# Norm and step sizes as one stage, with three of its pieces taken from the attention stage

## The chip, the cores and the metric

One core of a Trainium2 chip runs the whole kernel. The metric is the device time of one execution in microseconds (us). Times of work inside an execution come from one profiled execution of the same kernel, counted from the start of its span.

## The reference, cut to what matters

The kernel computes one layer of an encoder for two sequences (256 and 512 tokens, 768 in all, model width 1024), all in float32:

```python
h = rmsnorm(x, norm_mix)
proj = h @ w_in                     # 1024 x 8768
q, k, v, z, xbc, dt_f, dt_b, gate_a, gate_s = jnp.split(proj, split_points, axis=-1)
dt = jax.nn.softplus(dt_raw + dt_bias)
a_cum = jnp.cumsum(dt * a_head)     # per head, within chunks of 128 tokens, both directions
attn = window_attention(rope(q), rope(k), v, sink)
a_out = attn @ w_out_attn
s_out = ssd_branch(z, xbc, dt_f, dt_b, ...) @ w_out_ssm
x = x + (sigmoid(gate_a) * a_out + sigmoid(gate_s) * s_out) @ w_o
x = x + hier_moe(rmsnorm(x, norm_ffn), ...)
```

What matters here is the head of it: the norm `h`, the step sizes `dt` with their running sums, and when the columns of `w_in` are multiplied.

## The kernel before, in words

**Stages.** The program is a row of stages: norm and transpose, step sizes, the SSD scan (four groups), attention, the output projections, and the mixture of experts. Each stage is a block in which every engine has its own list of instructions, written out by hand in program order; engines wait for each other through semaphores only. A stage ends with a barrier of all engines. TensorE, VectorE (DVE), ScalarE (ACT), GpSimd (POOL) and SyncE (SP, which issues most DMAs) each run their list strictly in the order written, so an instruction that waits holds back all that is behind it.

**Pieces.** `w_in` is multiplied in pieces of 128 columns (512 KB). A piece is loaded by SP (`load_piece`), its rounded high part is made by ACT (`round_piece`, L518), its low part by POOL (`lower_piece`, L523), and TensorE then forms high by high, low by high and high by low for the eight blocks of 128 rows (`products`, L185): 24 matmuls for the 256 tokens of the first sequence and 24 for the 512 of the second. Three pieces are in flight (`RING`). TensorE waits for a piece's low part with `pieces.ready`. Pieces come in two kinds. Those of `xbc` feed the scan at once. Side pieces (q, k, v, z and the gates, 44 in all) are stored to the DRAM tensor `projected` and read later. Before, 33 of the 44 side pieces are computed in the SSD stage and 11 in the attention stage.

**Norm and transpose.** Six tiles of 128 tokens. Per tile, ACT sums squares (L262), POOL makes the root, DVE scales (`scaled`, L303), TensorE transposes eight 128x128 blocks into two banks of PSUM (L331), DVE multiplies by the gain (`norm_hT`, L317, one instruction for each half of the features), ACT rounds (`h_high`, L273) and POOL subtracts (`h_low`, L294).

**Step sizes.** A stage of its own, so it begins when the last tile has left POOL. TensorE multiplies the 64 step columns with `h` (L185, 48 matmuls), ACT copies the result (L410), six small transposes follow (L382), then DVE and ACT compute softplus and log (L437 to L448), TensorE forms the sums (L389 to L396), DVE copies them out (L454 to L463), and SP stores them to `decay_sums` (L369). The SSD stage waits for that store. The first three pieces of `xbc` are loaded, rounded and lowered beside this chain.

**Attention.** After an opening with rotary work, the loop runs over 24 groups (a tile and one of 4 key heads, 4 query heads each). In group g TensorE issues scores of group g+1 for two heads, then one third of a side piece (`unit`, L531: 24 matmuls of 256 columns or 12 of 512), then scores for the other two heads, then for each head of group g transposes of probabilities (L1233) and products with the values (L1183). Scores alternate between two banks, so a head waits until DVE has read the head two before it:

```python
                        if m >= 2:
                            pe.wait_ge(s_read, m - 1)
```

The 11 side pieces are 33 units: 9 in the opening and one in each of the 24 groups.

Of the kernel before, what the change touches and what calls it, by code (L numbers as in the profile page):

```python
# [14 lines left out]
P = 128  # L15
# [46 lines left out]
SIDES, LAST_SIDES = 9, 6  # L62
SSD_SIDES = (SG - 1) * SIDES + LAST_SIDES
# [161 lines left out]
def norm_and_transpose(core):  # L225
# [5 lines left out]
    AHEAD = 3  # L231
    with own:
# [5 lines left out]
        hT = [sb(f"norm_hT{u}", [P, 4, P]) for u in range(2)]  # L238
        x_in = [sem(f"x_in{n}") for n in range(len(LOADS))]
        const_in, mean_ok, rstd_ok = sem("const_in"), sem("mean_ok"), sem("rstd_ok")  # L240
        h_ok, tr_done, gained, high_ok, low_ok = (
            sem("h_ok"), sem("tr_done"), sem("h_gained"), sem("h_high_ok"), sem("h_low_ok"))
        with nc.Block() as block:

            @block.sync
            def _(sp):
# [5 lines left out]
                sp.dma_start(core.w_dt[:, :, :], core.w_in_cols(DT0, 2 * SH)).then_inc(core.w_dt_in, 16)  # L252

            @block.scalar
            def _(act):
# [9 lines left out]

                for t in range(AHEAD):
                    squares(t)
                for t in range(NT):
                    if t + AHEAD < NT:
                        squares(t + AHEAD)  # L270
                    for j in range(2):
                        act.wait_ge(gained, 2 * t + j + 1)
                        act.activation(core.h.high[:, 4 * j:4 * j + 4, t * P:(t + 1) * P], hT[j][:, :, :],  # L273
                                       ACT.Copy).then_inc(high_ok, 1)

            @block.gpsimd
            def _(pool):
# [10 lines left out]
                for t in range(NT):  # L288
                    if t + AHEAD < NT:
                        roots(t + AHEAD)  # L290
                    for j in range(2):
                        pool.wait_ge(high_ok, 2 * t + j + 1)
                        at = (slice(None), slice(4 * j, 4 * j + 4), slice(t * P, (t + 1) * P))
                        pool.tensor_tensor(core.h.low[at], hT[j][:, :, :], core.h.high[at].bitcast(F32),  # L294
                                           ALU.subtract).then_inc(low_ok, 1)

            @block.vector
            def _(dve):
# [8 lines left out]
                scaled(0)  # L307
                for t in range(NT):
                    if t + 1 < NT:
                        scaled(t + 1)  # L310
                    for j in range(2):
                        n = 2 * t + j
                        dve.wait_ge(tr_done, n + 1)
                        if n >= 2:
                            dve.wait_ge(low_ok, n - 1)
                        gain = core.feat[:, P_GMIX + 4 * j:P_GMIX + 4 * j + 4]
                        dve.tensor_tensor(hT[j][:, :, :], core.bank[n % 8][:, :].rearrange("p (k t) -> p k t", k=4),  # L317
                                          gain.unsqueeze(2).to_broadcast([P, 4, P]), ALU.mult).then_inc(gained, 1)

            @block.tensor  # L320
            def _(pe):
                pe.sem_inc(core.pieces.done, 2 * RING)
                pe.wait_ge(const_in, 16)
                for t in range(NT):
                    pe.wait_ge(h_ok, t + 1)
                    for j in range(2):
                        n = 2 * t + j
# [162 lines left out]
def piece_column(n):  # L490

    if n < GC:
        return xbc_column(0, n)
# [2079 lines left out]
```

## Time and profile before

| | us |
|---|---|
| median of 3 runs (2049.47 to 2055.22) | 2050.53 |
| the profiled execution | 2054.24 |
| its span, first to last instruction | 2052.4 |
| norm and transpose, until the step sizes start | 34.7 |
| step sizes, until the first matmul of the SSD stage | 63.26 |
| loop of attention | about 835 to 1026 |

The stage times are read from the order of the instructions in the trace. Outside the span of the profiled execution lie 1.84 us.

### The profile page before, as it was taken

The page shows a single profiled execution, that of the slowest core. Times are in us where ns is not written, and L with a number is a line of the kernel's source. Part 1 is how long each engine was busy: PE and PEld are TensorE (multiplying, and loading weights), DVE is VectorE, ACT ScalarE, POOL GpSimd, SP SyncE. Part 2 cuts the span into 40 slices and gives each one's busy share as a digit, 9 for nine tenths or more (in the row PEclk, how much of TensorE's full clock was granted, in tenths as well). Part 3 has the DMA queues.
Part 4 walks back from the last instruction along what each step waited for, and adds up shares of the span by engine and source line. Part 5 has one row for each costly group of instructions (what it writes and reads, how often), then busy time and mean ns, then how long its engine had stood idle before and what let it go on. Part 6 is the DMA issues. An engine that isn't in the chain of part 4 may idle for free. (4 is left out here: it accounts for less than half of the span.)

```text
span 2052.4 us, 26125 instructions
## 1 busy us (share of the span) xinstructions
PE 1842.6 (90%) x9426; PEld 1420.9 (69%) x9426; DVE 1283.2 (63%) x1351; ACT 1006.8 (49%) x1579; POOL 639.4 (31%) x368
## 2 busy tenths in 40 slices
PE   4898999999999779899999898985999999999991
PEld 3777787787787645677888786444677777777771
DVE  2677866875884835433344354124888888888883
ACT  4244543533444431355675420122577787777761
POOL 5247646746754933100134431000010111111000
PEclk7999999999999978899999999986999999999996
DMA  3243452424335442231155444512899999999985
GB/s 110 66 128 91 118 141 80 129 85 131 109 107 147 134 160 57 70 126 37 44 183 168 145 154 150 229 72 84 302 355 374 372 375 366 378 370 372 375 301 199
DMA packets 228110, 379.50 MB, mean 185 GB/s; under 512 B 14576, under 2 KB 176624, under 8 KB 203312
## 3 DMA queue, kind: packets, MB, share of 16 engines
q1 hardware_dynamic: 220272, 363.45, 51.8%
q0 software_dynamic: 7168, 12.60, 1.8%
q10 hardware_dynamic: 576, 2.18, 0.3%
q8 instruction: 61, 1.00, 0.2%
q14 instruction: 33, 0.27, 0.0%
HBM read 333.94 MB, written 55.25 MB: 190 GB/s over the span
## 5 line engine op out<-in xcount | busy, mean ns | idle before, releaser
L2011 DVE TENSOR_TENSOR e_w_low<-e_raw,e_w_high 128x2048 fp32r<-128x2048 f32 x190 | 426.5, 2286 | 63.3 <-ACT e_w_high L2007 63.3
L523 POOL TENSOR_TENSOR w_w_low<-w_raw,w_w_high 128x1024 fp32r<-128x1024 f32 x92 | 250.4, 2722 | 456.0 <-ACT w_w_high L518 456.0
L2007 ACT ACTIVATE e_w_high<-e_raw 128x2048 fp32r<-128x2048 f32 x190 | 349.9, 1914 | 0.0
L185 PE MATMUL bank<-h_high,w_w_high 128*128 128x512 f32 (+1 forms) x912 | 320.7, 352 | 31.9 <-ACT ssd_conv_in L802 16.7
L185 PE MATMUL bank<-h_low,w_w_high 128*128 128x512 f32 (+1 forms) x912 | 312.2, 342 | 0.0
L185 PE MATMUL bank<-h_high,w_w_low 128*128 128x512 f32 (+1 forms) x912 | 311.7, 342 | 0.0
L185 PEld LDWEIGHTS bank<-h_high,w_w_high 128*128 128x128 f32 x912 | 178.4, 196 | 65.0 <-issue 29.9
L2023 PE MATMUL bank<-e_w_high,e_xT_high 128*96 128x512 f32 x512 | 206.8, 404 | 3.2 <-DVE e_xT_low L2101 1.6
L2023 PE MATMUL bank<-e_w_high,e_xT_low 128*96 128x512 f32 x512 | 203.2, 397 | 0.0
L2023 PE MATMUL bank<-e_w_low,e_xT_high 128*96 128x512 f32 x512 | 202.3, 395 | 0.0
L946 DVE SCALAR_TENSOR_TENSOR ssd_xc<-ssd_conv_in,ssd_conv_p,ssd_xc 128x774 f32<-128x774 f32 x144 | 194.7, 1352 | 10.8
L2139 POOL DMA_INDIRECT y_rows<-e_y,slot_row x32 | 29.9, 933 | 524.1 <-ACT e_y L2073 510.5
L185 PEld LDWEIGHTS bank<-h_low,w_w_high 128*128 128x128 f32 x912 | 178.4, 196 | 18.8 <-issue 2.7
L185 PEld LDWEIGHTS bank<-h_high,w_w_low 128*128 128x128 f32 x912 | 178.2, 195 | 18.4
L822 ACT ACTIVATE ssd_decays<-ssd_decays,ssd_tabs 128x128 f32<-128x128 f32 x384 | 115.0, 389 | 142.4 <-DVE ssd_decays L954 142.4
L518 ACT ACTIVATE w_w_high<-w_raw 128x1024 fp32r<-128x1024 f32 x92 | 96.7, 1051 | 66.2 <-PE bank L185 61.2
L959 DVE TENSOR_TENSOR ssd_decays<-ssd_decays,ssd_cb 128x1024 f32<-128x1024 f32 x48 | 110.0, 2331 | 12.0 <-ACT ssd_decays L822 11.6
L2023 PE MATMUL bank<-e_w_high,e_hT_high 128*96 128x512 f32 x256 | 102.7, 401 | 10.3 <-DVE e_w_low L2011 10.3
L1366 DVE CUSTOM_DVE_ANT_0 att_buffers<-bank,late 128x256 f32<-128x256 f32 (+1 forms) x96 | 41.2, 467 | 112.8 <-PE bank L1169 112.8
L874 POOL TENSOR_TENSOR ssd_decays<-ssd_decays,ssd_tables 128x1024 f32<-128x1024 f32 x48 | 99.7, 2096 | 38.0 <-DMA ssd_decays<-decay_sums 38.0
L2023 PEld LDWEIGHTS bank<-e_w_high,e_xT_high 128*96 128x96 f32 x512 | 85.2, 167 | 35.3 <-issue 2.0
L2023 PEld LDWEIGHTS bank<-e_w_high,e_xT_low 128*96 128x96 f32 x512 | 83.2, 163 | 36.6 <-issue 0.3
(282 smaller groups left out, 3582.4 us busy)
## 6 DMA issues: line engine op xcount, KB each, us to landing
e_raw<-in_w_gate SPq DMA_DIRECT2D x64, 1024.0 KB, 7.6
e_raw<-in_w_up SPq DMA_DIRECT2D x64, 1024.0 KB, 7.6
e_raw<-in_w_down SPq DMA_DIRECT2D x64, 1024.0 KB, 6.9
w_raw<-in_w_in SPq DMA_DIRECT2D x68, 512.0 KB, 4.1
ssd_decays<-decay_sums SPq DMA_DIRECT2D x48, 512.0 KB, 6.6
projected<-ssd_side SPq DMA_DIRECT2D x33, 384.0 KB, 2.5
w_raw<-in_w_out_ssm SPq DMA_DIRECT2D x16, 512.0 KB, 4.1
y_ssd<-ssd_y SPq DMA_DIRECT2D x24, 256.0 KB, 2.4
```

The lines of the kernel that those rows point to most:

```text
L185: last = pe.matmul(out, lhs[k][a], rhs[k][b], start=(k == 0 and m == 0), stop=(k == n - 1 and m == 2))
L518: act.activation(self.pair[u].high[:, :, :], self.raw[u][:, :, :], ACT.Copy).then_inc(self.rounded, 1)
L523: pool.tensor_tensor(self.pair[u].low[:, :, :], self.raw[u][:, :, :], self.pair[u].high[:, :, :].bitcast(F32), ALU.subtract).then_inc(self ...
L822: last = act.activation(part, part, ACT.Exp, bias=gt["log_dt"][:, t, d, e:e + 1])
L874: last = pool.tensor_tensor(decays[t % NDEC][:, d, :, :], decays[t % NDEC][:, d, :, :], heads(table(g, "cum", t, d), P), ALU.subtract)
L946: last = dve.scalar_tensor_tensor(xc[:, ct, :], x[:, k:k + CONV], conv_p[:, ct, k:k + 1], xc[:, ct, :], ALU.mult, ALU.add)
L959: last = dve.tensor_tensor(decays[t % NDEC][:, d, :, :], decays[t % NDEC][:, d, :, :], cb[:, d, t, :].unsqueeze(1).to_broadcast([P, HPG, P ...
L1366: dve.tensor_tensor_reduce(score[g % 2][:, c, 0:n * P], core.bank[m % 2][:, 0:n * P], mask, 1.0, -3e38, ALU.add, ALU.max, top[:, t, h + c: ...
L2007: act.activation(pair[n].high[:, :], core.raw[c][:, :], ACT.Copy).then_inc(high_ok, 1)
L2011: dve.tensor_tensor(pair[n].low[:, :], core.raw[c][:, :], pair[n].high[:, :].bitcast(F32), ALU.subtract).then_inc(low_ok, 1)
L2023: done = pe.matmul(out, a[:, k0 + k, :], b[:, cols], start=(first and k == 0 and m == 0), stop=(last and k == ks - 1 and m == 2))
L2139: pool.indirect_dma_start(out=core.y_rows[:, :], out_offset=bass.IndirectOffsetOnAxis(ap=core.slot_row[:, e:e + 1], axis=0), in_=y[e % 2][ ...
```

## The change

Norm and step sizes become one stage, `front`, and three side pieces move into it from attention. 36 side pieces are then finished before attention, which has 8 (24 units): 9 in the opening as before, and 15 spread over the 24 groups, so that groups 0, 2, 5, 8, 10, 13, 16, 18 and 21 have none. The number of side pieces inside the SSD stage stays 33. The four stores that zero `y_rows` are issued together after the third side piece of attention instead of after the third to sixth. Six pieces are loaded in the front, not three.

In the front, the half tiles are split: POOL makes the first half of `h_low`, DVE the second. TensorE does the step product of the first sequence (`steps(0)`) after tile 2, and after each of tiles 3, 4 and 5 the first-sequence half of one side piece (`first(n)`). `steps(1)` follows, and the second-sequence halves (`second(n)`) stand in the chain of the step sizes.

```diff
-SIDES, LAST_SIDES = 9, 6
-SSD_SIDES = (SG - 1) * SIDES + LAST_SIDES
+FRONT, SIDES, LAST_SIDES = 3, 9, 6
+SSD_SIDES = FRONT + (SG - 1) * SIDES + LAST_SIDES
...
-def norm_and_transpose(core):
+def front(core):
...
+                for n in range(2 * RING):
+                    load_piece(sp, core, n)
+                for n in range(FRONT):
+                    sp.wait_ge(first_left, n + 1)
+                    sp.wait_ge(second_left, n + 1)
+                    sp.dma_start(core.projected[n * P:(n + 1) * P, :], side[n][:, :]).then_inc(side_out, 16)
+                    if n == FRONT - 2:
+                        sp.wait_ge(sumT_ok, 2)
+                        for d in range(2):
+                            sp.dma_start(core.sums[d], sumT[:, d, :]).then_inc(sumT_out, 16)
...
+                def first(n):
+                    core.pieces.ready(pe, n)
+                    products(pe, core.bank[FIRST_BANK[n]][:, 0:SEQS[0]], core.pieces.parts(n),
+                             h_parts(core, 0, SEQS[0])).then_inc(first_mm, 1)
+
+                def second(n):
+                    products(pe, core.bank[1 + n][:, 0:SEQS[1]], core.pieces.parts(n),
+                             h_parts(core, SEQS[0], SEQS[1])).then_inc(core.pieces.done, 2)
...
+                for t in range(NT):
+                    transposes(t)
+                    if t == 2:
+                        steps(0)
+                    if t > 2:
+                        first(t - 3)
+                steps(1)
+                second(0)
...
+                last.then_inc(dt_mm, 1)
+                second(1)
+                pe.wait_ge(a_ok, 1)
+                pe.wait_ge(first_left, FRONT)
+                pe.wait_ge(second_left, 1)
...
+                second(2)
...
+                def leave_second(n):
+                    core.pieces.finished(act, n, 1)
+                    act.activation(side[n][:, by_sequence(1)], core.bank[1 + n][:, 0:SEQS[1]], ACT.Copy)\
+                        .then_inc(second_left, 1)
+                    round_piece(act, core, n + RING)
...
+                    if 0 < t <= FRONT:
+                        round_piece(act, core, t - 1)
...
-                    for j in range(2):
-                        pool.wait_ge(high_ok, 2 * t + j + 1)
...
+                    pool.wait_ge(high_ok, 2 * t + 1)
+                    at = (slice(None), slice(0, 4), slice(t * P, (t + 1) * P))
+                    pool.tensor_tensor(core.h.low[at], hT[0][:, :, :], core.h.high[at].bitcast(F32),
+                                       ALU.subtract).then_inc(first_low_ok, 1)
+                    if t >= FRONT:
+                        lower_piece(pool, core, t - FRONT)
+                for n in range(FRONT):
+                    lower_piece(pool, core, n + RING)
...
+                    if t + 2 < NT:
+                        scaled(t + 2)
+                    dve.wait_ge(high_ok, 2 * t + 2)
+                    at = (slice(None), slice(4, 8), slice(t * P, (t + 1) * P))
+                    dve.tensor_tensor(core.h.low[at], hT[1][:, :, :], core.h.high[at].bitcast(F32),
+                                      ALU.subtract).then_inc(second_low_ok, 1)
...
-    OPENING = len(UNITS) - len(GROUPS)
+    OPENING = 9
+    REST = len(UNITS) - OPENING
+    UNITS_AT = [range(OPENING + g * REST // len(GROUPS), OPENING + (g + 1) * REST // len(GROUPS))
+                for g in range(len(GROUPS))]
...
-                    if 2 <= i < 2 + D // ZW:
-                        zeros(i - 2)
+                    if i == 2:
+                        for c in range(D // ZW):
+                            zeros(c)
...
-                            unit(OPENING + m // QPK)
+                            for u in UNITS_AT[m // QPK]:
+                                unit(u)
...
```

On TensorE in the front, the change puts the transposes of tile 4 (L298) between the first halves of two side pieces. These rows are around the end of `first(0)`, tile 4 and the start of `first(1)` (the L185 rows of `w_w` are a side piece's products):

```order
L185 MATMUL bank<-h_high,w_w_low 128x256
L298 MATMUL bank<-const,norm_h 128x128 [waits h_gained,h_ok]
L298 MATMUL bank<-const,norm_h 128x128 x3
L298 MATMUL bank<-const,norm_h 128x128 [waits h_gained]
L298 MATMUL bank<-const,norm_h 128x128 x3
L185 MATMUL bank<-h_high,w_w_high 128x256 [waits piece_split]
L185 MATMUL bank<-h_low,w_w_high 128x256
```

Before, the transposes of all six tiles followed one another with no product between them; now tile 4 stands behind the 24 products of `first(0)`, and `first(1)` behind a wait for POOL's `piece_split`.

On POOL before, from the root of the fifth tile to the end of the step sizes (`norm_mean` and `norm_rstd` are the root, `h_low` the subtraction for half a tile, `w_w_low` the low part of a piece):

```order
L294 TENSOR_TENSOR h_low<-norm_hT,h_high 128x4x128 [waits h_high_ok] x2
L201 TENSOR_SCALAR norm_mean<-norm_mean 128x1 [waits mean_ok]
L204 TENSOR_TENSOR norm_rstd<-norm_mean,const 128x1
L294 TENSOR_TENSOR h_low<-norm_hT,h_high 128x4x128 [waits h_high_ok] x8
L243 UNCONDITIONAL_BRANCH
L423 UNCONDITIONAL_BRANCH [waits barrier_Pool_Activation_PE_DVE_SP_gather]
L162 ISA x12
L523 TENSOR_TENSOR w_w_low<-w_raw,w_w_high 128x1024 [waits piece_rounded] x3
```

The same place in POOL's list after the change, to the end of the front:

```order
L436 TENSOR_TENSOR h_low<-norm_hT,h_high 128x4x128 [waits h_high_ok]
L201 TENSOR_SCALAR norm_mean<-norm_mean 128x1 [waits mean_ok]
L204 TENSOR_TENSOR norm_rstd<-norm_mean,const 128x1
L436 TENSOR_TENSOR h_low<-norm_hT,h_high 128x4x128 [waits h_high_ok] x2
L564 TENSOR_TENSOR w_w_low<-w_raw,w_w_high 128x1024 [waits piece_rounded]
L436 TENSOR_TENSOR h_low<-norm_hT,h_high 128x4x128 [waits h_high_ok]
L564 TENSOR_TENSOR w_w_low<-w_raw,w_w_high 128x1024 [waits piece_rounded]
L436 TENSOR_TENSOR h_low<-norm_hT,h_high 128x4x128 [waits h_high_ok]
L564 TENSOR_TENSOR w_w_low<-w_raw,w_w_high 128x1024 [waits piece_rounded] x4
```

The low part of the first side piece now stands behind the half tile of tile 3, the second behind tile 4, the third behind tile 5; three more pieces follow at the end.

On TensorE in attention after the change, group 0 (`k_both,qk` are scores, L1214; L1279 transposes probabilities, L1228 multiplies values):

```order
L1214 MATMUL bank<-k_both,qk 128x256 [waits qkv_x_used,qkv_k_copied]
L1214 MATMUL bank<-k_both,qk 128x256
L1214 MATMUL bank<-k_both,qk 128x256 [waits att_s_read] x6
L1279 MATMUL bank<-const,att_buffers 128x128 [waits att_p_ok]
L1279 MATMUL bank<-const,att_buffers 128x128
L1279 MATMUL bank<-const,att_buffers 128x128 [waits att_p_ok]
```

Before, 24 products of a unit stood between the fourth and the last two of those six score matmuls that wait for `att_s_read`; now the four scores of group 1 follow one another.

## Rows read from the trace of the kernel before

**Rows 1.** The page: busy time of TensorE, share of the span, instructions.

```profile
PE 1842.6 (90%) x9426; PEld 1420.9 (69%) x9426; DVE 1283.2 (63%) x1351; ACT 1006.8 (49%) x1579; POOL 639.4 (31%) x368
```

**Rows 2.** Windows: start:end, length, busy us of each engine, granted clock, DMA.

```profile
0.00:63.00 63.00, 28.09 (x132) 22.19 (x132) 20.53 (x34) 25.80 (x40) 29.00 (x32) 0.78 0.30 93
850.00:950.00 100.00, 100.00 (x688) 79.73 (x688) 35.67 (x166) 59.97 (x193) 9.45 (x4) 1.00 0.26 85
```

**Rows 3.** Timeline (start us, us, engine, line, work, [idle, releaser]): scores around an attention unit.

```profile
944.29 0.92 PE L1169 MATMUL bank<-k_both,qk 64*128 64x384 f32 x4
...
945.35 0.56 DVE L1366 CUSTOM_DVE_ANT_0 att_buffers<-bank,late 128x384 f32<-128x384 f32 x1 [4.17 <-PE bank L1169]
...
948.12 0.59 PE L1169 MATMUL bank<-k_both,qk 64*128 64x384 f32 x2
```

**Rows 4.** Timeline of TensorE: the start of the loop, around the unit of group 0.

```profile
838.86 1.56 PE L1169 MATMUL bank<-k_both,qk 64*128 64x256 f32 x4 [0.18 <-DVE att_top L1366]
840.35 0.58 PE L531 MATMUL bank<-h_high,w_w_high 128*128 128x256 f32 x1
...
845.68 0.49 PE L1169 MATMUL bank<-k_both,qk 64*128 64x256 f32 x2
```

**Rows 5.** Timeline: the first piece of the SSD stage, both halves, and ACT behind it.

```profile
63.26 0.36 PE L185 MATMUL bank<-h_high,w_w_high 128*128 128x256 f32 x1 [4.12 <-ACTq L852]
...
67.70 0.40 PE L185 MATMUL bank<-h_high,w_w_high 128*128 128x512 f32 x1
...
73.35 0.60 ACT L802 ACTIVATE ssd_conv_in<-bank 128x512 f32<-128x512 f32 x1 [4.98 <-PE bank L185]
73.84 1.05 ACT L518 ACTIVATE w_w_high<-w_raw 128x1024 fp32r<-128x1024 f32 x1
```

**Rows 6.** Timeline of POOL: the first half of tile 1.

```profile
18.83 1.61 POOL L294 TENSOR_TENSOR h_low<-norm_hT,h_high 128x512 fp32r<-128x512 f32 x1
```

**Rows 7.** Timeline: a tile's way from TensorE to POOL.

```profile
27.71 1.97 PE L331 MATMUL bank<-const,norm_h 128*128 128x128 f32 x8 [2.55 <-DVE norm_h L303]
...
28.90 0.69 DVE L317 TENSOR_TENSOR norm_hT<-bank,feat 128x512 f32<-128x512 f32 x1 [0.65 <-PE bank L331]
...
29.63 0.63 ACT L273 ACTIVATE h_high<-norm_hT 128x512 fp32r<-128x512 f32 x1 [0.71 <-DVE norm_hT L317]
...
31.79 2.61 POOL L294 TENSOR_TENSOR h_low<-norm_hT,h_high 128x512 fp32r<-128x512 f32 x2 [0.19 <-ACT h_high L273]
```

**Rows 8.** Timeline: a VectorE step beside a POOL low part, and that step's group.

```profile
83.31 2.82 POOL L523 TENSOR_TENSOR w_w_low<-w_raw,w_w_high 128x1024 fp32r<-128x1024 f32 x1 [5.26 <-ACT w_w_high L518]
...
83.94 3.01 DVE L946 SCALAR_TENSOR_TENSOR ssd_xc<-ssd_conv_in,ssd_conv_p,ssd_xc 128x774 f32<-128x774 f32 x1
...
L946 DVE SCALAR_TENSOR_TENSOR ssd_xc<-ssd_conv_in,ssd_conv_p,ssd_xc x36: 1024/1025/3008, 74.8 to 128.2; 128x774 f32<-128x774 f32 x36
```

**Rows 9.** Timeline of TensorE: first of the 24 step products of either sequence.

```profile
36.14 0.47 PE L185 MATMUL bank<-h_high,w_dt_high 128*64 128x256 f32 x1 [6.46 <-DVE w_dt_low L432]
...
40.70 0.39 PE L185 MATMUL bank<-h_high,w_dt_high 128*64 128x512 f32 x1
```

**Rows 10.** Timeline of POOL: low parts of three pieces.

```profile
40.27 7.11 POOL L523 TENSOR_TENSOR w_w_low<-w_raw,w_w_high 128x1024 fp32r<-128x1024 f32 x3 [5.87 <-ACT w_w_high L518]
```

**Rows 11.** Windows: columns as in rows 2; within the first half of that piece.

```profile
64.50:67.00 2.50, 2.50 (x14) 2.50 (x14) 0.00 (x0) 0.00 (x0) 0.00 (x0) 0.50 1.01 281
```

**Rows 12.** Timeline: the chain of the step sizes from its transposes to its sums.

```profile
47.06 0.46 PE L382 MATMUL bank<-const,dt_T 64*128 64x64 f32 x4 [0.42 <-ACT dt_T L410]
47.56 0.56 DVE L437 TENSOR_TENSOR dt_raw<-bank,row 128x384 f32<-128x384 f32 x1 [11.48 <-PE bank L382]
...
52.84 1.65 PE L389 MATMUL bank<-dt_a,const 128*128 128x192 f32 x4 [5.32 <-DVE dt_a L448]
...
55.70 3.44 PE L396 MATMUL bank<-const,dt_a 128*32 128x128 f32 x24
```

**Rows 13.** Timeline and waits of SP: the store that ends the step sizes.

```profile
60.22 0.83 SPq L369 DMA_DIRECT2D decay_sums<-dt_sumT  x2
...
SPq L361 <- DMA decay_sums<-dt_sumT: 1.5, 1, 1.5
```

More of the change, by code:

```diff
@@ L231, in norm_and_transpose @@
     AHEAD = 3
+    H2 = 2 * SH
+    FIRST_BANK = (6, 7, 5)
     with own:
@@ L274, in _ @@
                                        ACT.Copy).then_inc(high_ok, 1)
+                    if t == 0:
+                        act.wait_ge(core.w_dt_in, 16)
+                        act.activation(w_pair.high[:, :, :], core.w_dt[:, :, :], ACT.Copy).then_inc(w_high_ok, 1)
+                    if 0 < t <= FRONT:
+                        round_piece(act, core, t - 1)
+                    if t == NT - 2:
+                        step_parts(0)
+                act.activation(rate[:, :], core.row[:, R_ALOG:R_ALOG + H2], ACT.Exp).then_inc(rate_ok, 1)
+                for n in range(FRONT):
+                    leave_first(n)
+                step_parts(1)
+                leave_second(0)
+                act.wait_ge(raw_ok, 1)
+                act.activation(low[:, :, :], low[:, :, :], ACT.Exp)
+                act.drain()
+                act.activation(low[:, :, :], low[:, :, :], ACT.Ln, bias=core.ones[:, 0:1]).then_inc(soft_ok, 1)
+                act.wait_ge(dt_ok, 1)
+                act.activation(tab["log_dt"], tab["log_dt"], ACT.Ln)
+                leave_second(1)
+                act.wait_ge(exp_in_ok, 1)
+                for name in ("reach", "to_end", "decay"):
+                    last = act.activation(tab[name], tab[name], ACT.Exp)
+                last.then_inc(exp_ok, 1)
+                leave_second(2)
             @block.gpsimd
@@ L306, in _ @@
                 dve.wait_ge(core.params_in, 32)
-                scaled(0)
+                for t in range(2):
+                    scaled(t)
                 for t in range(NT):
-                    if t + 1 < NT:
-                        scaled(t + 1)
                     for j in range(2):
@@ L703, in scan @@
                     store(g, NT - 1)
-                for n in range(RING, GC + 2 * RING):
+                for n in range(2 * RING, FRONT + GC + 2 * RING):
                     load_piece(sp, core, n)
@@ L789, in _ @@
                 pe.sem_inc(y_mm, NT)
-                for n in range(GC):
+                for n in range(FRONT, FRONT + GC):
                     project(n, n % RING)
@@ L1309, in _ @@
                                 probabilities(m // QPK + 1)
-                            leave(OPENING + m // QPK)
+                            for u in UNITS_AT[m // QPK]:
+                                leave(u)
                     else:
```

246 lines of the change are left out of this document (107 added, 139 removed).

## The prediction

> **What bounds the kernel now.** The page comes first: TensorE is busy for 90% of the span [rows 1], so a change that only moves TensorE's work gains where TensorE is the bound at the old place and idle at the new one. The windows by stage say where that is. In the first 63 us TensorE is busy for 28.09 us and no engine for more than half of the time: chains bound the front. In attention's loop it is busy for all of 100 us at a granted clock of 1.00 (2.4 GHz), ACT for 60 and DVE for 36 [rows 2]. So TensorE's list sets the loop's pace, and what leaves it shortens the kernel, up to what other engines then make it wait. The question is what three pieces cost in the front, in program order.
>
> **What the move can return at most.** In the loop, scores begin at 944.29, a unit follows, and the next two scores begin at 948.12 [rows 3]. Two score heads take about 0.85 of that 3.83 (the first row's 0.92 overlaps the next instruction by some hundredths), so a unit takes 2.98. Nine go. The unit of group 0 runs before the clock has risen: 845.68 less 840.35, 5.33 [rows 4]. In full that would be 8 x 2.98 + 5.33 = 29.2 us.
>
> **What opens in its place.** A score head waits until DVE has read the head two before it. With a unit between, that is long over. Without it TensorE stands: DVE starts to read 1.06 us after the pair of scores starts, and takes 0.56 [rows 3]; with 0.06 to pass it on, the third head starts 1.68 after the first instead of 0.85, and the fourth waits some 0.06 more. At the loop's start, where no unit lies between the first pairs, the trace shows TensorE held by just this read [rows 4]. So a removed unit of a three-tile window returns 2.98 - 0.89 = 2.1; with two tiles reads are shorter, and I keep 2.1 for all eight: 16.8. In groups 5 and 10 ACT still has the copy and rounding of a side piece ahead of the copies that TensorE waits for (0.60 and 1.05, [rows 5]); I take off 0.6 for each: 15.6. Group 0 returns less than 5.33, because the half clock then falls on its other work and on the unit of group 1; I take 2.5, between 0 and 5.33. **Attention: -18.1**, between -14 (1.9 for each of eight less 1.2, group 0 nothing) and -29.2 (no wait opens).
>
> **The front, step by step.** I follow TensorE's new list from the third tile on.
>
> *steps(0)* needs both halves of `h_low` for tiles 0 and 1. POOL now makes the first half alone: 18.83 + 1.61 = 20.44 for tile 1 [rows 6]. The second half moves to DVE, one operation of 512 columns, 0.69 as its neighbour [rows 7]. When can it start? In the trace a DVE step with two inputs in SBUF, issued at 83.94 beside a POOL subtraction of 83.31 to 86.13, took 3.01, against a minimum of 1.02: it waited for POOL to end [rows 8]. So DVE subtracts from 20.44 to 21.13, and steps(0) starts at 21.2. It is 24 products: 40.70 - 36.14 = 4.56 before, after 6.46 idle [rows 9]. It ends at 25.8. Tile 3's transposes now stand behind it.
>
> *Tiles 3 to 5* become a ring. `first(n)` waits for POOL's low part of the piece, which stands in POOL's list behind the half tile of tile n + 3, which needs that tile's transposes; and the next tile's transposes stand behind `first(n)`. One round, from rows: transposes to DVE 1.19 (28.90 - 27.71), gain 0.69, to ACT 0.04, rounding 0.63, to POOL 0.07, half tile 1.31 (2.61/2) [rows 7], DVE's other half, which has waited for POOL and goes ahead of its next instruction, 0.69, low part of the piece 2.37 (7.11/3) [rows 10], to TensorE 0.13 (an estimate, between the 0.04 and 0.19 seen in the same rows), and 24 products. These come after TensorE has idled over 5 us. After 4.12 idle the first half of a piece took 67.70 - 63.26 = 4.44 [rows 5], with a granted clock of 0.50 (1.2 GHz) in the middle [rows 11]. The round is 11.56, three are 34.7: `first(2)` ends at 60.5. Before, the whole norm stage was over at 34.7.
>
> The 0.69 is a choice: rows show DVE waiting for POOL, not who goes next when both want to run. The Trainium skill ("SBUF — State Buffer", section "SBUF: two separate sides") states that the port pair shared by VectorE and GpSimd is locked for a whole instruction, not split, also for a DVE operation with two SBUF inputs against a GpSimd one that reads SBUF. By that rule both engines wait for each other, which is the sum as it stands; had POOL's next instruction never to wait, it would be 2.1 smaller. The trace agrees for DVE's wait (3.01 against 1.02).
>
> *The tail.* steps(1) has 24 products of 512 columns; 24 such take 73.35 - 67.70 = 5.65 [rows 5]. Then `second(0)` 5.65, and only then the six small transposes, 0.7 (0.46 for four, [rows 12]). `second(1)` 5.65 covers the chain to `a`, 52.84 - 47.56 = 5.28 [rows 12], so that chain costs nothing; were it longer, each us more would show. The sums took 52.84 to 59.14, 6.3 [rows 12]; behind `second(1)` TensorE comes without idle, and I take 5.3, with 6.3 as the bound. `second(2)` 5.65, then ACT's copy and rounding 1.54 (73.35 to 74.89, [rows 5]), then POOL's low part of the sixth piece, 0.1 + 2.4 [rows 10], which is what now ends the stage. The end of the stage took 0.7 after the store landed (60.22 + 0.83 + 1.5 = 62.55, to 63.26, [rows 5, 13]). Together 33.3: the SSD stage starts at 93.8 instead of 63.26. **Front: +30.5.**
>
> Bounds of the front: with the full clock throughout, steps(0) takes 2.8 (half of 5.65), each `first` 2.8, transposes some 0.3 less: -7.6; without the 0.69, -2.1; so +21. With half tile and low part as slow as when DVE holds POOL (1.61 and 2.82, [rows 6, 8]), 0.3 and 0.45 three times and 0.45 once, products at half clock to the end (5.1, +0.7 three times) and sums of 6.3: +5.8; so +36.
>
> **What costs nothing.** Three more loads in the front are 1.5 MB where the DMA engines are 30% busy [rows 2]; at 281 GB/s [rows 11] one takes 1.9 us, which is what it costs if late. The work of rounding pieces on ACT lies in ACT's idle time between tiles; `w_dt` is split while the ring has not begun. SP's fourth to sixth loads wait for POOL's first to third low parts, and the side stores behind them are due later than that; the store of the sums stands behind the second side store, which is issued before the sums are copied. The four zeroing stores, 6.3 MB, occupy SP's queue for 22 us at the same rate; the next transfer that anyone waits for comes about four groups later, and were it in the way, it would cost ACT the rest of those 22. The SSD stage keeps its 33 side pieces and its order.
>
> **The sum.** +30.5 - 18.1 = +12.4 on the profiled execution's 2054.24, so 2066.6 for one like it; that execution lies 3.7 above the median of the runs shown, and against the median 2050.53 the forecast is **2063**: slower. About 0.3% (6.2 us) is what a measurement of this kernel can tell from no change.
>
> **Rivals.**
> - *The units return all of their time* (not slower). If TensorE does not stand between the score pairs, attention returns 29.2 and the sum is +1.3: 2052. It decides from 2.7 us returned for each of the nine, (30.5 - 6.2)/9. For it: the loop is TensorE-bound to the last tenth [rows 2]. Against: the 1.06 + 0.56 of DVE's read [rows 3], and the wait at the loop's start [rows 4].
> - *The clock stays up* in the front. Then the ring is 7.6 shorter: +4.8, 2055, no change to speak of. For it: more work in the front. Against: each `first` follows over 5 us of idle, and after 4.12 the clock fell to half [rows 5, 11].
> - *The pieces lie in idle time.* If `first(n)` did not hold the next tile, three rounds would take some 5 us each as a tile did before: 20 us less, and with attention -7.6: 2043, faster. The order of instructions speaks against it: the wait for `piece_split` stands ahead of the next transposes.
> - *Another chain paces the loop without units.* ACT was busy for 60 of 100 us [rows 2]; if each removed unit returns only 1 us, attention gives -9 and the sum is +21: 2072.
>
> **Chances and range.** Forecast 0.57 (2057 to 2069); full return 0.10; clock up 0.14; idle time 0.06; another pace 0.13. Slower: 0.56 of the forecast, 0.12 of the last and 0.04 of the clock case, 0.72; same: 0.20, mostly of full return and the clock; faster: 0.08, the idle-time case and the fast edge of full return. The range 2051 to 2070 leaves out the idle-time case, the fast half of full return and most of the slow case.
>
> **What would show it.** In the changed kernel's profile: the first matmul of the SSD stage at about 94 (61 would kill the ring); transposes of tiles 4 and 5 some 11.6 apart, with TensorE idle 5 to 6 us before each `first`, ended by POOL's low part; POOL's sixth low part as the last work of the front; the loop of attention 18 us shorter, with TensorE held by DVE's read twice in nine groups. The forecast is wrong if the ring's round is under 8 us, or if the loop shrinks by more than 25.

## The result and the profile after

| | before | after |
|---|---|---|
| median of 6 runs | 2052.40 (2049.47 to 2055.22) | 2064.36 (2062.12 to 2068.31) |
| the profiled execution: time, span | 2054.24, 2052.4 | 2063.79, 2061.7 |
| first matmul of the SSD stage | 63.26 | 89.71 |
| SSD stage, to the first unit of attention | 683.13 | 687.87 |
| attention's opening, to the first score | 89.01 | 83.95 |
| attention's loop, to the last output transposes | 190.26 | 175.27 |
| the rest | 1026.74 | 1024.90 |

The changed kernel takes 1.0061 times as long (95% interval 1.0048 to 1.0074). That is about 12.5 us more by this ratio, and 12.0 by the two medians: a small change, but slower and clear of the noise, and 2064.4 where 2063 was forecast. The span grew by 9.3 in the two profiled executions: +26.45 (front), +4.74, -5.06, -14.99 and -1.84, in the order of the table's last five rows.

The page of the changed kernel, the line that answers to [rows 1]:

```profile
PE 1843.1 (89%) x9426; PEld 1427.7 (69%) x9426; DVE 1296.8 (63%) x1357; ACT 1006.9 (49%) x1579; POOL 631.4 (31%) x362
```

TensorE has the same 9426 matmuls and the same busy time. Nothing was saved or added there; what changed is where it waits. The windows of the changed kernel (columns as in [rows 2]):

```profile
0.00:89.70 89.70, 53.59 (x276) 46.03 (x277) 29.60 (x40) 30.87 (x49) 29.86 (x29) 0.87 0.31 96
63.26:89.70 26.44, 21.81 (x111) 17.39 (x109) 8.13 (x15) 10.69 (x15) 7.08 (x3) 0.96 0.15 53
880.00:980.00 100.00, 94.96 (x670) 75.54 (x669) 39.85 (x178) 63.75 (x206) 7.07 (x3) 1.00 0.11 33
```

The front holds 25.5 us more of TensorE's work than before (53.59 less 28.09) and takes 26.45 longer: almost nothing of the three pieces lies in its idle time. In attention's loop TensorE was busy for 100 of 100 us and now is for 95: the pieces left, and waits came.

TensorE's timeline in the front: the first step product, the first product of each side piece, the transposes of tiles 4 and 5 between them, and the start of the SSD stage.

```profile
20.72 0.44 PE L185 MATMUL bank<-h_high,w_dt_high 128*64 128x256 f32 x1 [4.38 <-DVE h_low L468]
32.47 0.58 PE L185 MATMUL bank<-h_high,w_w_high 128*128 128x256 f32 x1 [5.49 <-POOL w_w_low L564]
37.09 1.03 PE L298 MATMUL bank<-const,norm_h 128*128 128x128 f32 x8
43.22 0.58 PE L185 MATMUL bank<-h_high,w_w_high 128*128 128x256 f32 x1 [5.10 <-POOL w_w_low L564]
47.63 1.03 PE L298 MATMUL bank<-const,norm_h 128*128 128x128 f32 x8
53.76 0.58 PE L185 MATMUL bank<-h_high,w_w_high 128*128 128x256 f32 x1 [5.10 <-POOL w_w_low L564]
89.71 0.55 PE L185 MATMUL bank<-h_high,w_w_high 128*128 128x256 f32 x1 [4.64 <-ACTq L893]
```

That is the ring as forecast: each side piece begins after 5.1 to 5.5 us of idle that POOL's low part ends, and the next tile's transposes stand behind it, 10.54 apart. One round of it on the other engines (tile 4), and the last work of the front:

```profile
37.73 1.29 DVE L462 TENSOR_TENSOR norm_hT<-bank,feat 128x512 f32<-128x512 f32 x2 [7.51 <-PE bank L298]
38.45 1.23 ACT L392 ACTIVATE h_high<-norm_hT 128x512 fp32r<-128x512 f32 x2 [8.97 <-DVE norm_hT L462]
39.16 1.27 POOL L436 TENSOR_TENSOR h_low<-norm_hT,h_high 128x512 fp32r<-128x512 f32 x1 [6.74 <-ACT h_high L392]
39.71 1.26 DVE L468 TENSOR_TENSOR h_low<-norm_hT,h_high 128x512 fp32r<-128x512 f32 x1 [0.69 <-ACT h_high L392]
40.38 2.79 POOL L564 TENSOR_TENSOR w_w_low<-w_raw,w_w_high 128x1024 fp32r<-128x1024 f32 x1
...
86.72 2.34 POOL L564 TENSOR_TENSOR w_w_low<-w_raw,w_w_high 128x1024 fp32r<-128x1024 f32 x1 [7.33 <-ACT w_w_high L559]
```

DVE's half (39.71) takes 1.26, where the same instruction takes 0.69 when it starts ahead of POOL's (tile 0 in e6, at 15.04). POOL's low part takes 2.79, and 2.34 with DVE out of the way (86.72). Each waits for the other for about half a microsecond.

Attention, a group without a unit, with scores over two tiles of keys (880) and over three (953). [rows 3] show a group with three tiles and its unit before.

```profile
880.34 0.70 PE L1214 MATMUL bank<-k_both,qk 64*128 64x256 f32 x4
...
881.19 0.42 DVE L1413 CUSTOM_DVE_ANT_0 att_buffers<-bank,late 128x256 f32<-128x256 f32 x1 [2.02 <-PE bank L1214]
...
881.67 1.04 PE L1214 MATMUL bank<-k_both,qk 64*128 64x256 f32 x4 [0.63 <-DVE att_top L1413]
...
952.99 0.92 PE L1214 MATMUL bank<-k_both,qk 64*128 64x384 f32 x4
954.66 1.39 PE L1214 MATMUL bank<-k_both,qk 64*128 64x384 f32 x4 [0.76 <-DVE att_top L1413]
```

The second pair of scores starts 1.33 or 1.67 after the first, ended by DVE's read. The 0.63 or 0.76 that the view calls idle is not all: the second pair also takes 1.04 in place of 0.70 (1.39 in place of 0.92), since its second head waits for DVE's second read, and the view counts that as busy.

### The profile page after: what moved, and what is told of

It is laid out like the page before. It is cut to its first block and busy times, and to the rows that moved or that the text cites. A ratio compares the mean times of both kernels' runs of the same rounds, so it can differ in the third digit from the quotient of the medians.

```text
span 2061.7 us, 26121 instructions
## 1 busy us (share of the span) xinstructions
PE 1843.1 (89%) x9426; PEld 1427.7 (69%) x9426; DVE 1296.8 (63%) x1357; ACT 1006.9 (49%) x1579; POOL 631.4 (31%) x362
## 5 line engine op out<-in xcount | busy, mean ns | idle before, releaser
L185 PE MATMUL bank<-h_high,w_w_high 128*128 128x256 f32 (+1 forms) x960 | 340.1, 354 | 48.2 <-ACT ssd_conv_in L843 16.7
L185 PE MATMUL bank<-h_low,w_w_high 128*128 128x256 f32 (+1 forms) x960 | 330.8, 345 | 0.0
L185 PE MATMUL bank<-h_high,w_w_low 128*128 128x256 f32 (+1 forms) x960 | 330.2, 344 | 0.0
L185 PEld LDWEIGHTS bank<-h_high,w_w_high 128*128 128x128 f32 x960 | 190.5, 198 | 82.9 <-issue 25.6
L185 PEld LDWEIGHTS bank<-h_low,w_w_high 128*128 128x128 f32 x960 | 190.4, 198 | 19.4 <-issue 2.6
L185 PEld LDWEIGHTS bank<-h_high,w_w_low 128*128 128x128 f32 x960 | 189.9, 198 | 19.3
L2070 PEld LDWEIGHTS bank<-e_w_low,e_xT_high 128*96 128x96 f32 x512 | 83.6, 163 | 32.1
```

What stands on the lines that cost most here:

```text
L185: last = pe.matmul(out, lhs[k][a], rhs[k][b], start=(k == 0 and m == 0), stop=(k == n - 1 and m == 2))
L2070: done = pe.matmul(out, a[:, k0 + k, :], b[:, cols], start=(first and k == 0 and m == 0), stop=(last and k == ks - 1 and m == 2))
```

## The experiments

Stages of every kernel that ran, from its profiled execution (first SSD matmul; lengths of the SSD stage, of attention's opening and loop), and its time against the kernel before. The median of the kernel before was 2050.4 beside e1 to e4, 2052.5 beside e5 to e7 and 2054.4 beside e8 to e10, so kernels of different groups are compared by the ratio. Stage lengths are of one execution each. The rest after attention, which no edit touches, took between 1020.9 (e6) and 1028.6 (e9), so a single difference of 2 or 3 us between stages can be chance where no row shows its cause.

| | SSD at | SSD | opening | loop | median | ratio, 95% interval |
|---|---|---|---|---|---|---|
| e1_low_first | 72.03 | 683.24 | 85.36 | 180.73 | 2048.2 | 0.9984 (0.9967 to 1.0001) |
| e2_last_group | 63.48 | 691.87 | 86.84 | 175.16 | 2044.3 | 0.9967 (0.9951 to 0.9983) |
| e3_conv_first | 90.73 | 684.09 | 88.19 | 175.18 | 2062.1 | 1.0053 (1.0037 to 1.0069) |
| e4_half_back | 94.67 | 685.90 | 88.21 | 175.17 | 2069.8 | 1.0080 (1.0054 to 1.0105) |
| e5_apart | 90.83 | 684.41 | 89.91 | 176.68 | 2064.2 | 1.0054 (1.0037 to 1.0072) |
| e6_merge | 62.08 | 693.97 | 88.66 | 175.18 | 2040.8 | 0.9942 (0.9922 to 0.9961) |
| e7_merge_apart | 61.29 | 691.73 | 83.17 | 176.74 | 2040.2 | 0.9938 (0.9920 to 0.9956) |
| e8_merge_defer | 62.27 | 691.63 | 86.92 | 170.68 | 2037.4 | 0.9921 (0.9905 to 0.9937) |
| e9_low_defer | 71.63 | 684.21 | 86.48 | 170.75 | 2041.4 | 0.9939 (0.9922 to 0.9956) |
| e10_defer | 90.38 | 684.34 | 89.96 | 174.72 | 2065.0 | 1.0053 (1.0035 to 1.0072) |

**e1, the ring broken at one link.** On POOL:

```diff
-                    if t >= FRONT:
-                        lower_piece(pool, core, t - FRONT)
+                    if FRONT - 1 <= t < NT - 1:
+                        lower_piece(pool, core, t - FRONT + 1)
```

> The changed kernel, with POOL's low part of side piece n one place earlier in its list: ahead of the half tile of tile n + 3 and no longer behind it. Theory (the ring): the low part was the link that tied a piece to the tile behind which it stands, so TensorE now goes from the transposes straight into first(n). A round falls from 10.6 us to 4.2 to 6.4 (transposes 1.4 to 2, 24 products 2.8 at the full clock to 4.6 at half), three rounds give back 13 to 19, the first matmul of the SSD stage stands at 71 to 77 in place of 89.7, and the time is 2045 to 2051. Rival (a tile's own chain over DVE, ACT and POOL sets the round, about 5 us for a tile in the kernel before, with the products behind it): a round stays at 8 to 10, the front gives back 2 to 8, the time is 2056 to 2062.

TensorE's timeline in the front of e1: the transposes of tiles 3 to 5 (the view's window ended within the last), the one piece that still waits, and the start of the SSD stage.

```profile
26.36 1.41 PE L298 MATMUL bank<-const,norm_h 128*128 128x128 f32 x8
30.47 1.04 PE L298 MATMUL bank<-const,norm_h 128*128 128x128 f32 x8
33.30 0.39 PE L185 MATMUL bank<-h_high,w_w_high 128*128 128x256 f32 x1 [1.79 <-POOL w_w_low L564]
36.27 0.93 PE L298 MATMUL bank<-const,norm_h 128*128 128x128 f32 x7
...
72.03 0.55 PE L185 MATMUL bank<-h_high,w_w_high 128*128 128x256 f32 x1 [4.64 <-ACTq L893]
```

Rounds of 4.1 and 5.8, the SSD stage 17.7 earlier: the ring it was, and the rival falls. All of the work is still there, so the +26 of the front were some 9 net for the pieces and 18 of waiting in a ring. The time is 2048.2, as the theory had it (2045 to 2051): about 16 less than the changed kernel, and not to be told from the kernel before. In the profiled execution the loop took 180.73, 5.5 more than with the same instructions elsewhere. How many of the other executions had this, no run shows. The windows of e1 say why:

```profile
911.00:916.00 5.00, 3.52 (x21) 2.50 (x20) 2.98 (x9) 4.68 (x13) 1.59 (x1) 0.86 0.19 79
916.00:924.00 8.00, 8.00 (x36) 6.81 (x36) 3.02 (x10) 3.20 (x12) 0.75 (x1) 0.50 0.22 66
924.00:930.00 6.00, 6.00 (x46) 4.94 (x44) 1.44 (x7) 2.05 (x7) 0.00 (x0) 0.93 0.01 3
```

TensorE stood for 1.5 of 5 us in group 10 (the scores' 0.63, then 0.86 for ACT), and for the next 8 us its granted clock was 0.50 (1.2 GHz).

**e2, attention's part alone**, with the pieces in the last SSD group (and the kernel before's two stages):

```diff
-SIDES, LAST_SIDES = 9, 6
+SIDES, LAST_SIDES = 9, 9
...
-LAST_STEP_SIDES = ((3,), (4,), (5,), (), (), ())
+LAST_STEP_SIDES = STEP_SIDES
```

> The kernel before, with its two separate stages at the front, and the attention of the changed kernel: the three side pieces that left attention stand in the last three steps of the last SSD group, where the kernel before has none. It tells attention's part from the front's. Theory: attention's loop is as in the changed kernel, 175 us in place of 190, and its first stages are unchanged (first SSD matmul at 63). In the last group the steps with a piece took 12.8 us and the three without 10.6, 8.4 and 11.2, so the SSD stage grows by 8 to 12, and the sum against the kernel before is -3 to -7: 2045 to 2049. Rival one (the pieces pay in full wherever they stand, 25 us for three): 2062. Rival two (the 5 us that attention's opening was shorter are the change's and not the clock's): another 5 less, 2040 to 2044.

The loop is 175.16, so attention's part does not hang on the front. The SSD stage grew by 8.7 for the same three pieces that cost 26 in the front, because TensorE had room there. A window of the kernel before, in the last but one step of that group:

```profile
726.80:735.20 8.40, 5.04 (x18) 3.92 (x18) 7.61 (x9) 4.78 (x16) 4.73 (x3) 0.66 0.08 31
```

And one of e2 in the same part of the stage:

```profile
725.00:735.00 10.00, 9.30 (x57) 8.00 (x56) 9.85 (x7) 3.67 (x13) 10.00 (x5) 1.00 0.29 93
```

TensorE was busy for 60% of it at a granted clock of 0.66; with the pieces it is for 93%, at 1.00. The kernel is faster than before by 0.33%, 6.1 us by the medians, as the theory's sum said (3 to 7).

**e3, POOL held back at the start of the SSD stage.** The profile after had shown 3 us lost there:

```diff
                     lower_piece(pool, core, FRONT + n + RING)
+                pool.wait_ge(conv_done, GC + 2)
                 groups(pool, scan)
```

> The changed kernel, with one wait more on POOL at the start of the first SSD group: its differences begin only when DVE has finished the convolutions of that group. Theory (in the profile of the changed kernel POOL starts them at 154.61, just ahead of DVE's last convolution step, which then waits some 1.5 us for POOL; ACT, then TensorE are late, and TensorE's clock falls to half; in the kernel before POOL started just behind that step): the SSD stage loses the 3.1 us that arose there, 688 to about 685, and the time is 2061. Rival (the 3 us are the granted clock's, not POOL's): the stage stays at 687 to 688, or grows by the 0.8 to 2.6 us by which POOL starts later.

The stage lost 3.8. But e5 and e10, which have the changed kernel's front without this wait, have 684.41 and 684.34 as well. The changed kernel's timeline (DVE, POOL, TensorE):

```profile
149.72 8.00 DVE L987 SCALAR_TENSOR_TENSOR ssd_xc<-ssd_conv_in,ssd_conv_p,ssd_xc 128x774 f32<-128x774 f32 x6
154.61 4.86 POOL L915 TENSOR_TENSOR ssd_decays<-ssd_decays,ssd_tables 128x1024 f32<-128x1024 f32 x2 [7.71 <-DMA ssd_decays<-decay_sums]
158.65 2.52 PE L792 MATMUL bank<-ssd_xc 128*128 128x128 f32 x12 [3.02 <-ACT ssd_xc L856]
```

DVE and POOL in e10:

```profile
149.65 6.52 DVE L987 SCALAR_TENSOR_TENSOR ssd_xc<-ssd_conv_in,ssd_conv_p,ssd_xc 128x774 f32<-128x774 f32 x6
155.20 4.58 POOL L915 TENSOR_TENSOR ssd_decays<-ssd_decays,ssd_tables 128x1024 f32<-128x1024 f32 x2 [8.37 <-DMA ssd_decays<-decay_sums]
```

POOL began some 0.6 before the last of DVE's six steps was due, so the six took 8.00 where they take 6.52 undisturbed; TensorE idled 3.02 in place of 1.55, and its granted clock fell to 0.50. In e5 and e10 POOL began when that step had just begun (0.67 and 0.97 before its end; it takes 1.02), and nothing was late. So the mechanism holds and the cause is a chance: POOL starts when a load of `decay_sums` has landed. From its issue to its landing that load took 7.14 in this execution, and 7.77 to 8.24 in those of the kernel before and of all ten experiments. With the usual landing the wait is worth 0.3, which is within chance, and not 3. The median of e3, 2062.1, cannot be told from the changed kernel's (the intervals overlap).

**e4, DVE's half tile back on POOL**, with POOL doing both halves:

```diff
+                    pool.wait_ge(high_ok, 2 * t + 2)
+                    at = (slice(None), slice(4, 8), slice(t * P, (t + 1) * P))
+                    pool.tensor_tensor(core.h.low[at], hT[1][:, :, :], ...)
...
-                    dve.wait_ge(high_ok, 2 * t + 2)
...
```

> The changed kernel, with the second half tile of h_low back on POOL, behind the first, as before the change. Theory of the prediction (a round holds 0.69 us of DVE's half, which POOL waits for): that goes, 1.31 us of POOL's second half comes, +0.6 for each of three rounds, and steps(0) and steps(1) start up to 1.3 later: SSD starts 2 to 4 us later, time 2066 to 2068. Rival (DVE's half costs the ring nothing, since POOL need not wait for it): +1.3 in each round and the same at steps(0), SSD 5 us later, 2069. Rival (DVE's half is what stretches POOL's low part from 2.35 to 2.79 and its half tile from 1.3 to 1.66): 0.8 of each round comes back, and the sum is 1 us or less.

POOL's timeline for tile 4 in e4:

```profile
41.22 1.26 POOL L436 TENSOR_TENSOR h_low<-norm_hT,h_high 128x512 fp32r<-128x512 f32 x1 [7.51 <-ACT h_high L392]
...
42.44 1.26 POOL L440 TENSOR_TENSOR h_low<-norm_hT,h_high 128x512 fp32r<-128x512 f32 x1
43.66 2.34 POOL L564 TENSOR_TENSOR w_w_low<-w_raw,w_w_high 128x1024 fp32r<-128x1024 f32 x1
```

The low part is 2.34 again, 0.45 less, and 1.22 of second half stand before it; rounds became 12.3 and 11.4. The SSD stage starts 3.8 to 5.0 later than in the four kernels with the changed front (89.71 to 90.83), 4.1 later than their median. That lies between the first theory's 2 to 4 and the first rival's 5, so the sum does not part them. The rows do: DVE's half does hold POOL's low part, as the theory had it, but for 0.45 and not 0.69. The last rival is out.

**e5, the stand between scores removed.** In groups without a unit, the second pair of scores moves behind the first head:

```diff
-                            if more:
+                            if more and UNITS_AT[m // QPK]:
                                 scores(m // QPK + 1, range(2, QPK))
+                        if m % QPK == 1 and more and not UNITS_AT[m // QPK]:
+                            scores(m // QPK + 1, range(2, QPK))
```

> The changed kernel, with one change in attention: in the nine groups without a unit the second pair of scores of the next group stands behind the first head's transposes and values, and no longer right behind the first pair. Theory (what a removed unit does not give back is TensorE's stand until DVE has read a score): the 0.63 to 0.76 us of idle TensorE between the pairs go, 9 times, the loop is 169 to 170 in place of 175.2, and the time some 6 below the changed kernel's 2062 to 2064: 2056 to 2058. Rival (the later scores make ACT's exponentials late, and the next group's first transposes wait instead): the loop stays at 174 to 177. Rival (the loop without units is paced by ACT's and DVE's own chain): no change in the loop, idle time of TensorE in other places.

The stands between the score pairs of groups without a unit are all gone, and the loop did not shrink: 176.68, in the range of the first rival, though not for its reason. The timeline of e5 shows where they went:

```profile
935.28 1.05 ACT L559 ACTIVATE w_w_high<-w_raw 128x1024 fp32r<-128x1024 f32 x1
...
936.22 1.06 ACT L1361 ACTIVATE mergedT<-bank 128x512 f32<-128x512 f32 x2
...
936.86 0.69 PE L1281 MATMUL bank<-const,att_buffers 128*128 128x128 f32 x2 [2.53 <-ACT mergedT L1361]
```

TensorE came earlier to a place where ACT has the rounding of a piece ahead of the output copies, and stood 2.53 instead of 0.86. From 935 to 945 its granted clock was 0.59. From DVE's last read of a score in group 10 to that in group 12 it took 19.77 (9.25 and 10.52), in place of 14.37 (5.47 and 8.90) in the changed kernel: 5.4 us, more than the new place of the scores had given (some 4: the loops of e8 and e10 below, which differ in attention by that place alone).

**e6, the merge without the pieces**: the merged front, with no product of a side piece in it, and the pieces where e2 has them (the edit is the removal of `first`, `second` and their waits, with `FRONT = 0`, `LAST_SIDES = 9`).

> The changed kernel with the three side pieces taken out of the merged front and put in the last SSD group, as in e2. It tells what merging the two stages is worth by itself, against e2 with its two stages. Theory (the change's loss is the pieces' ring alone, the merged stage is a gain): steps(0) runs from 21 to 26 between the tiles, steps(1) can start when tile 5 is split, at 34 to 35, takes 5.7 to 8, chain and sums as before: the first SSD matmul stands at 57 to 59 in place of 63.3, all else as in e2, 2038 to 2041. Rival (the merged order delays tiles 3 to 5 behind steps(0) by its 4.6 to 5.4 us, and nothing is won): SSD at 62 to 64, 2044.

By the stages the rival was right: SSD at 62.08, 1.2 to 2.2 before the two stages of e2 (e6, e7 and e8: 62.08, 61.29, 62.27). The median, 2040.8, is where the theory had it and not at the rival's 2044, but no stage that the edit touches shows why: the first unit of attention starts at 756.05, in e2 at 755.35, and the rest after attention, 4 us shorter than in e2, is not the edit's. The intervals of the two ratios overlap, so whether the merge by itself wins anything is not shown. TensorE in e6 at the second step product:

```profile
36.73 0.66 PE L185 MATMUL bank<-h_high,w_dt_high 128*64 128x512 f32 x1 [7.05 <-DVE h_low L424]
```

steps(0) between tiles 2 and 3 makes tile 5 late, so steps(1) starts at 36.7 and not at 34 to 35, after 7 us of idle. The SSD stage of e6 is 2.1 longer than that of e2; I did not find out why, and e7 and e8, with the same pieces there and e3's wait besides, are nearer to e2.

**e7, all of these together** (e6 with the edits of e5 and e3).

> e6 with the score order of e5 and the wait of e3: the candidate that all three theories give. Sum: e2's 2044.3, less 5 for the merged front, less 6 for the scores, less 0 to 3 in the first SSD group: 2031 to 2035. If the scores give nothing, 2038; if the merge gives nothing as well, 2043.

2040.2, not 2031 to 2035: the loop was 176.74, with the same stand of 2.53 and a fall of the clock behind it as in e5. What was left open was whether ACT's 2.53 started it.

**e8, ACT's order at that place**, on top of e7: a side piece's copy and rounding wait until the output copies are done.

```diff
-                            for u in UNITS_AT[m // QPK]:
-                                leave(u)
+                            if PLAN[r + 1][0] == "probs":
+                                for u in UNITS_AT[m // QPK]:
+                                    leave(u)
...
+                        if j == 1:
+                            for u in UNITS_AT[PLAN[r - 2][3] // QPK]:
+                                leave(u)
```

> e7 with one change more, in ACT's list in attention: where the copies of a finished output tile follow a group, they now go ahead of the copy and rounding of a side piece (this meets in group 9, and at the end). In e5 and e7 the stands between the scores were gone, but TensorE then stood 2.53 us for ACT's output copies behind that rounding, and its clock fell to half for two groups, which took 9.3 and 10.5 us instead of 7.5 and 6.9. Theory (these 2.53 us started the fall): with the output copies first TensorE stands below 1 us there, the clock stays, the loop is 169 to 171 in place of 176.7, and the time is 2032 to 2036. Rival (ACT's whole chain is the bound there, and TensorE waits at the next copy as long): the loop stays at 175 to 177, 2040.

TensorE in e8 at the place of e5's 2.53:

```profile
911.05 0.44 PE L1238 MATMUL bank<-const,att_buffers 128*128 128x128 f32 x2 [1.10 <-ACT mergedT L1319]
```

1.10, no fall of the clock (1.00 from 905 to 915), 13.89 from the last read of group 10 to that of group 12 (by that mark the changed kernel has 5.47 and 8.90, not the 7.5 and 6.9 of the expectation; the sum is the same), and a loop of 170.68: the first theory for the loop. The time is 1.4 above the 2032 to 2036 that it gave. The ratio is the lowest of the study, 0.79% below the kernel before, but its interval overlaps with those of e6, e7 and e9. What tells e8 from e7 is the loop: it fell to half clock in both profiled executions with the 2.53 (e5, e7) and in neither with the 1.10 (e8, e9). These are two against two, and e1 shows that a fall also comes without that stand, so chance is unlikely here but not excluded.

**e9, the pieces in the front after all**, with e1's order, e3's wait and both edits of attention:

> The pieces in the front as the change has them, with the ring broken as in e1, and the wait of e3 and the two edits of attention of e8. It tells whether three pieces are better off in the merged front or in the last SSD group, with all else alike. Front as in e1 (72), SSD stage 683 to 685, loop 169 to 171 by the first theory of e8: 2034 to 2039, within 3 us of e8. If the clock falls in the loop all the same, 2041 to 2045.

Loop 170.75, front 71.63, SSD stage 684.21: each stage as expected. First SSD matmul and SSD stage together are 755.84 here and 753.90 in e8. That these 2 us are the place's is not shown: e6, e7 and e8, with the pieces in the same place, have 756.05, 753.02 and 753.90. The median is 2041.4, above the expected 2034 to 2039 and 4 above e8's, where 3 was expected: the rest after attention was 1028.6 in the profiled execution, against 1026.0 in e8 and 1024.7 to 1024.9 in e10 and the changed kernel, and no edit touches it. Which place is better stays open.

**e10, ACT's order alone** on the changed kernel:

> The changed kernel with ACT's order of e8 alone. It sizes the prediction's term for the rounding on ACT (0.6 us for each of two groups). Theory: only group 10 shows it, TensorE's 0.86 us of idle there goes, the loop is 174.3 to 174.6 in place of 175.2, the time that of the changed kernel less 1: 2061 to 2064. Rival (the copy of the piece now delays the exponentials or the low part of the next piece): the loop stays or grows by 1.

TensorE at that place in the changed kernel:

```profile
934.86 0.44 PE L1279 MATMUL bank<-const,att_buffers 128*128 128x128 f32 x2 [0.86 <-ACT mergedT L1359]
```

And in e10:

```profile
938.70 0.44 PE L1279 MATMUL bank<-const,att_buffers 128*128 128x128 f32 x2 [0.24 <-ACT att_buffers L1351]
```

TensorE's 0.86 became 0.24, and the loop 174.72, 0.55 less than in the changed kernel: just under the theory's 0.6 to 0.9. The median, 2065.0, is 1 above the expected range and too coarse to show it. By itself this wait was worth half a microsecond; its weight came with e5.

## Why the prediction was right, point by point

- **The front, +30.5: right in mechanism, some 3 too large.** Measured +26.45; +27.3 with the median of the four kernels that have this front (90.55). steps(0) ran from 20.72 to 26.07 where 21.2 to 25.8 was worked out.
- **The round, 11.56: measured 10.75 and 10.54.** Two terms were too large. The transposes' 1.19 came from a stretch at half clock; here it was 0.64 (37.73 less 37.09), the granted clock being 1.00 in that stretch. And the 0.69 for DVE's half was 0.45 in POOL's row. The Trainium skill ("SBUF — State Buffer", section "SBUF: two separate sides") states that the port pair is held by one of VectorE and GpSimd for a whole instruction. The trace agrees with it in both directions: DVE's 1.26 and POOL's 2.79, and 2.34 in e4 where no DVE half is near. Counted back from its end at 40.97, DVE's 0.69 began at 40.28, and POOL's low part was issued at 40.38: so DVE had already run for 0.1 (an estimate from these rows). That is part of the 0.24 by which the term was too large; what the rest is, no row shows.
- **The tail, 33.3: measured 31.7** (from the first product of steps(1), at 58.03, to 89.71). The sums took 4.2 (75.21 to 79.41) and not 5.3; that is most of it. POOL's sixth low part was the last work, as forecast.
- **Attention, -18.1: measured -15.0**, and the loop is between 175.16 and 175.27 in all five kernels with this loop and no fall of the clock in it (the changed kernel, e2, e3, e4, e6). Two steps failed. One is the fourth head's "some 0.06 more": it waits 0.34 with two tiles and 0.47 with three. A group's stand is then 0.97 (five groups) or 1.23 (three), 8.5 in sum, so eight units return 8 x 2.98 - 8.5 = 15.3, not 16.8. The other is group 0, where 2.5 was taken between 0 and 5.33. The scores of group 3 begin 18.81 after the first score (880.34 less 861.53), and 20.04 before, so group 0 returned 1.2: the half clock then fell on the unit of group 1, which took 4.55 (872.54 to 877.09). ACT in group 10 cost 0.86 where 1.2 was taken off. The remaining 0.7 lies spread over the eight groups; I did not trace it.
- **What costs nothing** held: in the loop ACT, POOL and SP wait for no transfer, so the four stores together cost nothing that the trace shows, though they fill the DMA engines for 20 us (a busy share of 1.02 and 1.01 in the first two windows of 10 us).
- **The SSD stage keeps its order, at no cost: nearly.** 4.74 longer in the profiled execution; in e5 and e10 with the same front 1.2 to 1.3, the cause of which stays open. The rest is chance: about 3 us arose where POOL's early start held DVE's last convolution step.
- **Attention's opening, not spoken of**, was 5.06 shorter. It was 88.2 to 90.0 in e3, e5 and e10, which share all of it, and 89.01 before: not the change's. What shortened it in this execution and in e7 (83.17) stays open.
- **The sum.** Both large terms were too large by some 3, and the errors cancelled: +27.3 - 15.0 + 1.2 is +13.5, where 12.4 was forecast and 12.5 measured. So the nearness of 2063 to 2064.4 is partly luck. The median that the forecast was counted from also moved, from 2050.53 to 2052.40 with six runs.
- **The rivals.** Full return is out (the loop would be 161). The clock did not stay up (steps(0) ran at a granted clock of 0.51, the first halves of the three pieces at 0.59, 0.63 and 0.65). That the pieces lie in idle time is false of this order and, after e1, two thirds true of another. That another chain paces the loop without units was false here; but e5 shows ACT's chain close behind, ready to take over.

## What to carry to other kernels

Work that is moved into idle time must not wait for something that stands behind the next piece of the chain it is put into: one instruction's place on POOL was worth 18 us here. The last SSD group, where TensorE had room, cost 9 for the same pieces in place of 26, and so did the front with the ring broken. When filler is taken out of a saturated loop, count what it covered, per group and with the second-order wait that a view books as busy. After each repair look for the next wait in the row, since removing one stand can bring TensorE early to a longer one.

## What the runs showed of the hardware that I had not expected

A stand of 2.53 us in a loop that is otherwise dense (e5, e7), or of 0.63 and 0.86 within 3 us (e1), was followed by 8 to 10 us in which the granted clock fell to 0.50 (1.2 GHz); in e5 it cost 5.4, in e1 4.5 over the same two groups. The same 0.63 and 0.86 were not followed by a fall in the changed kernel (granted clock 1.00 from 934 to 960), and 1.10 and 1.20 were not in e8 (1.00 from 905 to 925 and from 972 to 982). So the length of a short stand alone did not settle whether it cost its length or several times as much.
